# Recurrence of an RWKV layer: crossed factor products on four squares of the array, and a step's order staggered by groups of four tiles

## The reference

```python
def wkv_scan(r, decay, k, v, a_vec, b_vec, s0, reverse):
    def step(s, inp):
        r_t, w_t, k_t, v_t, a_t, b_t = inp
        sa = jnp.einsum('bhvk,bhk->bhv', s, a_t)
        s = s * w_t[:, :, None, :] + sa[..., None] * b_t[:, :, None, :] + v_t[..., None] * k_t[:, :, None, :]
        return s, jnp.einsum('bhvk,bhk->bhv', s, r_t)
...
for d in range(N_DIRS):
    reverse = d == 1
    yc_d, s_ctx = wkv_scan(r_c, dec_c, k_c, vh_c, -kk_c, kk_c * a_c, s0, reverse)
    yx_d, _ = wkv_scan(r_x, dec_x, k_x, vh_x, -kk_x, kk_x * a_x, s_ctx, reverse)
```

## Time and profile before

| | |
|---|---|
| three runs | 3694.95, 3694.49, 3689.80 us; median 3694.49 |
| profiled execution | 3690.83 us, span of its trace 3689.0 us, granted clock 0.98 |
| busy in the span | TensorE 3437.3 us (93%), weight loads 2264.5 (61%), VectorE 1475.1 (40%), ScalarE 1100.6 (30%), GpSimd 320.7 (9%) |
| chain that ended last | TensorE 76%, VectorE 10%, DMA 8%, ScalarE 3%, GpSimd 2% |
| recurrence | from about 1283 to 1776 us of the span |

### The profile page before, as it was taken

One profiled execution on the slowest core, in us unless ns is written; L12 is line 12 of the kernel. 1 busy time (PEld: TensorE's weight loads), 2 busy tenths in 40 slices (PEclk: granted clock), 3 DMA queues, 4 the chain that ended last, 5 costly groups with the idle time before them and its releaser, 6 DMA issues.

```text
span 3689.0 us, 64299 instructions
## 1 busy us (share of the span) xinstructions
PE 3437.3 (93%) x28700; PEld 2264.5 (61%) x28700; DVE 1475.1 (40%) x2584; ACT 1100.6 (30%) x2075; POOL 320.7 (9%) x264
## 2 busy tenths in 40 slices
PE   6999999999899999999778887899999999999998
PEld 4555344335558588888443332266888876878886
DVE  2133001013642277777540000157753435674343
ACT  3121111113442255544210000144532323543131
POOL 0001000000100234443110000001000001000000
PEclk9999999999799999999989999999999999999999
DMA  8237988996434334332528999920243312133320
GB/s 343 92 138 277 375 333 330 380 346 247 159 121 155 108 81 97 74 72 50 183 108 368 421 414 421 420 83 28 65 148 95 99 41 76 41 126 103 91 91 23
DMA packets 340516, 666.55 MB, mean 181 GB/s; under 512 B 156600, under 2 KB 250296, under 8 KB 284944
## 3 DMA queue, kind: packets, MB, share of 16 engines
q1 hardware_dynamic: 330128, 633.14, 47.8%
q10 hardware_dynamic: 6912, 18.88, 1.4%
q0 software_dynamic: 3200, 10.42, 0.8%
HBM read 630.92 MB, written 31.46 MB: 180 GB/s over the span
## 4 chain that ended last, share of the span: by engine, by line
PE 76%; DVE 10%; DMA 8%; ACT 3%; POOL 2%; issue 1%; SPq 0%; DVEq 0%; ACTq 0%; POOLq 0%
PE ps L1074 14%; PE ps L1079 5%; DMA ring<-in_moe_wu 4%; PE ps L716 4%; PE ps L3205 3%; PE ps L3204 3%; PE ps L3203 3%; PE ps L3221 3%; PE ps L3222 3%; PE ps L3220 3%; PE ps L632 3%; PE ps L633 3%; PE ps L634 2%; PE ps L1509 2%; PE ps L1534 2%; POOL ring L1899 2%
## 5 line engine op out<-in xcount | busy, mean ns | idle before, releaser
L1074 PE MATMUL ps<-ring,H 128*64 128x512 f32 x2016 | 482.8, 600 | 43.4 <-DMA ring<-in_moe_wu 33.0
L1185 DVE TENSOR_TENSOR scr<-ps,scr 128x512 f32<-128x512 f32 x32 | 22.1, 692 | 901.0 <-PE ps L1079 495.6
L1074 PEld LDWEIGHTS ps<-ring,H 128*64 128x64 f32 x2016 | 147.2, 137 | 321.9 <-issue 230.1
L1074 PE MATMUL ps<-ring,scr 128*64 128x512 f32 x1016 | 246.2, 601 | 31.2 <-DMA ring<-in_moe_wd 27.2
L3185 DVE TENSOR_TENSOR ring_rounded<-ring,scr_rounded 128x2048 fp32r<-128x2048 f32 x64 | 146.7, 2293 | 216.6 <-ACT scr_rounded L3178 216.3
L3220 PE MATMUL ps<-scr_rounded,ring_rounded 128*128 128x512 f32 x512 | 201.8, 394 | 1.6 <-DVE ring_rounded L3185 1.6
L3203 PE MATMUL ps<-scr_rounded,ring_rounded 128*128 128x512 f32 x512 | 202.8, 396 | 0.0
L3205 PE MATMUL ps<-scr_rounded 128*128 128x512 f32 x512 | 202.6, 396 | 0.0
L3222 PE MATMUL ps<-scr_rounded 128*128 128x512 f32 x512 | 202.4, 395 | 0.0
L3204 PE MATMUL ps<-H_rounded,scr_rounded 128*128 128x512 f32 x512 | 202.3, 395 | 0.0
L3178 ACT ACTIVATE scr_rounded<-ring 128x2048 fp32r<-128x2048 f32 x64 | 122.2, 1909 | 242.7 <-PE ps L3222 242.7
(11 more groups left out here) (524 smaller groups left out, 6793.2 us busy)
## 6 DMA issues: line engine op xcount, KB each, us to landing
ring<-in_moe_wu SPq DMA_DIRECT2D x128, 1024.0 KB, 9.2
ring<-in_moe_wd SPq DMA_DIRECT2D x127, 1024.0 KB, 9.5
ring<-in_moe_wg SPq DMA_DIRECT2D x124, 1024.0 KB, 9.2
ring<-in_mlp_w SPq DMA_DIRECT2D x64, 1024.0 KB, 5.4
ring<-in_ada_w SPq DMA_DIRECT2D x48, 1024.0 KB, 10.5
ring<-in_w_in SPq DMA_DIRECT2D x14, 1024.0 KB, 5.3
ring<-in_w_out SPq DMA_DIRECT2D x8, 1024.0 KB, 5.2
st_kka<-scr ACTq DMA_DIRECT2D x16, 384.0 KB, 3.5
```

What stands on the lines that cost most here:

```text
L1074: ins = pe.matmul(bx[64 * n:64 * n + 64, :], stat_x(k), w[:, k % 4, :], start=k == 0, stop=k == KT - 1)
```

## The change

It has four parts, all in the recurrence.

1. **Four squares.** `factor` on TensorE takes both units of a step together, tile by tile, and writes the reverse unit's product to the other half of the partitions (`rows(q ^ d)`): the forward unit stays on one diagonal of the array, the reverse unit goes to the other. ScalarE uncrosses it with two copies of 64 partitions.
2. **Groups.** Every call takes one group g for both units. In a level the order is factor of group 0, another product, update of group 0, factor of group 1, another product, update of group 1. The other products (outputs, states, keys, score products) come in halves; right side and solution stand first in the step.
3. **Scan, exponentials, operands.** CS has a second buffer (`CS1`) for odd units from u = 3 on. The first exponential (`chunk_rise`) and the second (`chunk_fall`) have their own marks, and so have the operands that read EP (`chunk_readers`) and those that are written with EN (`chunk_writers`). The scans move ahead: one to the start of the step, one to the end of level 1.
4. **The engines' own orders** follow: additions and transposes of VectorE by group for both units, the decay between the two halves of level 2, masked copies in pairs of banks, copies of ScalarE by group.

The core of the diff (waits of unchanged form are left out):

```diff
-            def factor(pair, l):
+            def factor(pair, l, g):
+                both = []
                 for u, d, c, img, first in pair:
...
+                    both.append((u, d, b))
+                for j in range(4 * g, 4 * g + 4):
+                    o = slice((j % 4) * CH, (j % 4) * CH + CH)
+                    for u, d, b in both:
+                        for q in range(2):
+                            ins = pe.matmul(b[rows(q ^ d), o], NM[d][l][rows(q), j, :], XT[d][rows(q), j, :],
                                             start=True, stop=True)
-                        did(T_, ins.then_inc(tensor_done, 1), f"G{u}.{l}.{g}")
+                        if j == 4 * g + 3:
+                            did(T_, ins.then_inc(tensor_done, 1), f"G{u}.{l}.{g}")
...
         def wkv_scalar(act):
+            def factor(pair, l, g):
+                for u, d, c, img, first in pair:
+                    t = pairs(tile(act, f"G{u}.{l}.{g}"))
+                    out = GT[d][:, 4 * g:4 * g + 4, :]
+                    if d == 0:
+                        did(A_, act.activation(out, t, ACT.Copy).then_inc(scalar_done, 1), f"free.G{u}.{l}.{g}")
+                    else:
+                        did(A_, act.activation(out[rows(0)], t[rows(1)], ACT.Copy).then_inc(scalar_done, 1))
+                        did(A_, act.activation(out[rows(1)], t[rows(0)], ACT.Copy).then_inc(scalar_done, 1), f"free.G{u}.{l}.{g}")
...
+                right_side(before, 0)
+                right_side(before, 1)
+                solution(before, 0)
+                factor(now, 1, 0)
+                solution(before, 1)
+                factor(now, 1, 1)
                 if after:
+                    chunk_rise(act, *after[0])
+                    chunk_fall(act, *after[0])
+                factor(now, 2, 0)
...
+                    chunk_rise(act, *after[1])
+                factor(now, 2, 1)
+                factor(now, 3, 0)
...
+                factor(now, 3, 1)
...
+                    keys(*now[1])
                 if after:
+                    chunk_fall(act, *after[1])
+                factor(now, 4, 0)
+                if after:
+                    chunk_evict(act, *after[0], (0,))
...
+        def csum(u):
+            return CS1 if u >= 2 and u % 2 else CS0
...
+        def chunk_readers(dve, u, d, c, img, first):
+            ld = LD[:, d]
+            if later(dve, f"rise{u}"):
+                dve.wait_ge(*at(f"rise{u}"))
...
+            did(V, dve.scalar_tensor_tensor(r[:, :, 0, :], v3(ld[:, 2, :]), -1.0, EM[d], ALU.mult, ALU.mult).then_inc(vector_done, 1))
+            if img:
+                did(V, dve.tensor_tensor(r[:, :, 1, :], v3(ld[:, 5, :]), EP[d], ALU.mult).then_inc(vector_done, 1))
+            e = CH - 1 if d == 0 else 0
+            did(V, dve.tensor_copy(PT[:, u % 4, :], EP[d][:, :, e]).then_inc(vector_done, 1))
...
+                right_side(before, 0)
+                right_side(before, 1)
+                solve(before, 0)
+                solve(before, 1)
+                factor(now, 1, 0)
+                factor(now, 1, 1)
+                outputs(image, 0)
+                update(now, 1, 0)
+                outputs(image, 1)
+                update(now, 1, 1)
+                factor(now, 2, 0)
+                states(before, 0)
+                update(now, 2, 0)
...
+                factor(now, 4, 0)
                 if after:
-                    chunk_products(pe, *after[0])
-                factor(now, 5)
-                update(now, 5)
+                    chunk_products(pe, *after[0], (0,))
+                update(now, 4, 0)
+                factor(now, 4, 1)
                 if after:
-                    chunk_products(pe, *after[1])
+                    chunk_products(pe, *after[0], (1,))
+                update(now, 4, 1)
...
```

More of the change, by code:

```diff
@@ L1981, in chunk_products @@
             w = 128 if img else CH
-            for g in range(2):
+            for g in groups:
                 for q in range(2):
@@ L2014, in solution, with keys @@
                     marks[f"free.S{u}.{g}"] = (A_, count[A_])
+            def keys(u, d, c, img, first):
+                for q in range(2):
+                    t = tile(act, f"T{u}.{q}")
+                    did(A_, act.activation(odd(BKT[d], q), t.rearrange("p (h c) -> p h c", c=CH), ACT.Copy).then_inc(scalar_done, 1), f"free.T{u}.{q}")
             steps = list(units())
@@ L2160, in keys @@
-            def keys(pair):
-                for u, d, c, img, first in pair:
-                    for q in range(2):
-                        b = bank(pe, f"T{u}.{q}")
-                        for j in range(8):
-                            ins = pe.transpose(b[:, j * CH:j * CH + CH], BK[d][rows(q), j, :, :], ident[rows(q), rows(q)])
-                        did(T_, ins.then_inc(tensor_done, 1), f"T{u}.{q}")
-            def right_side(pair):
+                    b = bank(pe, f"P{u}.{l}.{g}")
@@ new lines, in update @@
+                    if later(pe, f"free.G{u}.{l}.{g}"):
+                        pe.wait_ge(*at(f"free.G{u}.{l}.{g}"))
+                    if later(pe, f"xi{u}.{l - 1}.{g}"):
+                        pe.wait_ge(*at(f"xi{u}.{l - 1}.{g}"))
+                    for j, q, o in each(g):
+                        ins = pe.matmul(b[rows(q), o], GT[d][rows(q), j, :], x[rows(q), j, :],
+                                        start=True, stop=True)
+                    did(T_, ins.then_inc(tensor_done, 1), f"P{u}.{l}.{g}")
@@ L2169, in right_side, with keys @@
+            def keys(u, d, c, img, first):
+                for q in range(2):
+                    b = bank(pe, f"T{u}.{q}")
+                    for j in range(8):
+                        ins = pe.transpose(b[:, j * CH:j * CH + CH], BK[d][rows(q), j, :, :], ident[rows(q), rows(q)])
+                    did(T_, ins.then_inc(tensor_done, 1), f"T{u}.{q}")
+            def right_side(pair, g):
                 for u, d, c, img, first in pair:
@@ L2217, in states @@
-            def states(pair):
+                    b = ybank[u]
+                    if later(pe, f"free.S{u}.{g}"):
+                        pe.wait_ge(*at(f"free.S{u}.{g}"))
+                    for j, q, o in each(g):
+                        if later(pe, f"free.A{u}.{2 * g + q}"):
+                            pe.wait_ge(*at(f"free.A{u}.{2 * g + q}"))
+                        ins = pe.matmul(b[rows(q), o], sv[q][:, j, :], sc[:, 2 * j + q, CH:2 * CH],
+                                        start=False, stop=j == 4 * g + 3)
```

341 lines of the change are left out of this document (166 added, 175 removed).

## The result

The changed kernel takes 3673.9 us (median of 7 runs, 3667.0 to 3682.0) against 3694.5 of the kernel before in the same series: ratio 0.995, 95% interval 0.9939 to 0.9961. It is faster by 20 us (14 to 23 by the interval); forecast were 40, with 3654 in place of 3673.9. The direction was right and the time inside the range; the size was off by a factor of two.

The account below looks back on a forecast made before the run. TensorE was taken to set the recurrence's step, VectorE next. 55 saved on factor blocks less 12 for borders and 1 for waits is 42, shaded to 40 for scans: 3654 us, range 3632 to 3686.

Parts of the forecast that it names:

- Four squares, 55 saved: Factor products on TensorE: 120 blocks fall from 0.98 to 0.52 us each, 55 us saved, ends 0 and 59.
- feed of 25 ns: Rival, factor blocks: passes fed no faster than 25 ns, a block takes 0.80 us, 3665 us in all; chance 0.16.
- bank rule: Factor products: row halves cannot write one PSUM bank together, so no gain there; two-squares rival 3685 us, chance 0.09.
- Borders 12: TensorE, recurrence: some 110 more borders between kinds of product at 0.11 us each, 12 us lost, ends 0 and 15.
- waits 36: TensorE's waits in the new order: 36 us over twelve steps against 34.7 today, 1 lost; ends 22 gained, 40 lost.
- bank wait of 1.3: Level 4's second updates wait 1.3 us a step for first-score-product banks that VectorE's masked copies free.
- Loads and scans: Scans at a step's start: loads have 11 us left to land, cost nothing; scans beside masks nothing, other end 26 us.
- Twelve equal steps: Recurrence: blocks counted as 120 over twelve steps, waits as 2.9 a step, some 3.2 in context steps.
- cover of the crossed copies: ScalarE's 120 more copies, 4.0 us a step, are hidden by updates and filler, except level 1 of context steps.
- The lock: Rival: VectorE's six operand products, slipping beside GpSimd's masks, take 1.07 us extra each, 3731 us; chance 0.04.

Follow-up runs that it names:

- two squares: Changed kernel's order with both units' factor products on one diagonal and one ScalarE copy for two, against the changed kernel: 3688.3 us, ratio 0.999.
- First scans late: Changed kernel with VectorE's scans behind level 2 and level 3, ScalarE's exponentials behind them, in step 0 alone: 3670.1 us, ratio 0.9941.
- the loads issued first as well: Changed kernel with step 0's scans moved back and the second step's loads issued ahead of the 1 MB of weights: 3665.5 us, ratio 0.9928.
- last pairs: Changed kernel with levels 4 and 5 of the last step run as factors, factors, updates, updates: 3674.3 us, ratio 0.9949.
- solve between: Changed kernel with the second half of the solve between level 1's two factor blocks in image steps: 3680.2 us, ratio 0.9965.
- scans late in all steps: Changed kernel with the scans behind level 2 and level 3, exponentials behind them, in every step: 3709.1 us, ratio 1.0044.
- one alone: Kernel before, in its order, with only the factor products interleaved on both diagonals and ScalarE's crossed copies: 3713.4 us, ratio 1.0056.

## Why the forecast was right in direction and wrong in size

*Four squares, 55 saved.* The pace was as forecast. From the last pass of the updates ahead to the first of the next line, a block takes 0.61 us, and 1.08 with two squares in the same order: 0.47 saved where 0.46 was forecast, though the 32 passes mostly start within 0.52 us and not within 0.5. The rivals by a feed of 25 ns and by the bank rule are both out: two units' products write both halves of two banks at this pace. The term's worth was overstated: ten blocks give TensorE 4.7 us a step, and the steady step is 1.5 shorter. Two squares in the new order were to cost 31 us more (3685 for 3654) and cost 14.4. What the blocks no longer take, TensorE waits: 0.5 us of an image step of 40.9 are not busy with two squares, 1.9 of 38.9 with four.

*Borders 12, waits 36.* The stagger was understated. Two squares in the new order were to gain 0.8 a step (waits from 34.7 to 13, less 12 for borders) and gain 1.8 in an image step. A border is as forecast, 0.15 us from a line's last pass to the next line's first against a pace of 0.03. The two errors cancel, which is luck, and the steady step came out at 39.35 where 39.2 was forecast; the walk's bank wait of 1.3 is 0.8 in the trace, and its 0.3 to 0.7 elsewhere 0.4 to 0.6. TensorE's 37.0 busy us were put at 35, which is 39.5 less 4.6 for the blocks and leaves out the ten more borders of the forecast's own sum, 1.1.

*Loads and scans: here the forecast failed.* "I cost them at nothing" looked at a steady step. In step 0 the loads that the next scans read are issued only as the recurrence begins, and the scan now stands ahead of level 1's additions, which nothing of these loads concerns:

```profile
DVE scr L1960 <- DMA H<-st_kk: 12.1, 2, 11.6
```

In the kernel before, VectorE waited 2.3 us for that load:

```profile
DVE scr L1945 <- DMA H<-st_kk: 2.3, 1, 2.3
```

"First scans late" takes the wait out of the first stretch, but shows no gain clear of noise; with the loads issued first as well, the medians give 8.4 us and the profiled recurrence 4.6. So 5 to 8 us of this term's loss are shown by a run. The stretch itself is 9.1 us longer than before.

*Twelve equal steps.* The last step has no products of a next one to stand between. Four waits of 0.48 for ScalarE (1.9 us), stops of 1.10 and 1.53, and a clock at half for one stretch (0.88 over its second half) outweigh the shorter blocks: 4.2 us more. Its own experiment, last pairs, did not shorten it, so how these share the loss is open. The cover of the crossed copies was claimed for every step but level 1 of the context steps.

*The account.* 42 us for twelve steps are 3.5 a step. The first and the last stretch together make one step: counted as 3.5 less, they are 9.1 + 4.2 = 13.3 more, 16.8 of the 21.5 that are missing. The four context intervals were to give 14.0 and gave 10.2, the seven image ones 24.5 and gave 23.5; that is the other 4.8.

*VectorE and GpSimd.* The lock is real and hit other operations than those named. The six operand products take 0.65 to 0.68, as forecast, also L1957's, which took 1.22 in the mean before. The scans went from 1.22 to 1.60 us in the mean and the identity's add from 1.21 to 1.49; a decay beside the masks took up to 1.77. What the steady step pays for it is not shown: taking the scans out from beside the masks brought waits for ScalarE that cost more. In the context steps TensorE waited for transposes behind the decay.

*What was not foreseen at all.* Late code: 8 us more of stops than before, in 18 stops where there were 3. They lie inside the intervals of the account and are no further term. That they take part of what another edit gives is likely, but their sum also varies by 6 us between kernels with the same products.

*Left open.* TensorE's clock in the context steps. The changed kernel's profile shows 0.95 in one of them. Two variants whose instructions there are its own, last pairs and solve between, show 0.80 in the third interval, which lasts 43.1 us for 37.1:

```profile
1369.70:1412.80 43.10, 39.49 (x995) 37.40 (x993) 28.90 (x57) 26.05 (x66) 20.76 (x15) 0.80 0.35 77
```

0.80 lies between the two levels of 1.2 and 2.4 GHz: part of the interval ran at the lower. Just ahead of it TensorE had waited 2.15 us there, and 1.98 in the other variant, for VectorE's transposes, where the changed kernel waited 0.77; two squares, whose waits in these steps are 1.0 at most, stayed at 1.00. That makes the waits the likely cause, and it would account for the spread of the runs (15 us for the changed kernel, 6 before). It was not tested by itself.

## What to carry to other kernels

Do not multiply a steady step: walk the first and the last one of a loop by themselves, and for each instruction moved ahead ask when its inputs arrive in the first. A faster block of products pays only as far as other work stands between it and the engines that read it; measure both halves of such a change alone, since here one alone lost 21 us, the other alone gained 4, and together they gained 20. When TensorE stops with nothing to wait for at matmuls whose numbers lie at equal distances, look at its code.

## What the runs showed of the hardware

- Four 64x64 squares of the array run at once over whole blocks: four fp32 passes start each 0.06 us, 15 ns a pass, for 32 passes (0.48 to 0.52 us), with two banks written in both halves of the partitions. The Trainium skill's page "TensorE: Matmul & The Clock Gate" (section "Wait — 56ns, not 53.3ns?") says that start-to-start never drops below about 25 ns; across squares, this trace says otherwise.
- TensorE's code comes in pieces of 16 KB, some 126 matmuls (with their weight loads) each, and TensorE stops for 0.2 to 2.5 us when a piece lands late. It goes on 1.2 to 1.8 us after the landing (once 2.8). The recurrence has 2.3 us of such stops before and 4.4 with two squares, but 8.2 to 16.9 in the variants that have both the four squares and the new order, apart from scans late in all steps, which is slower and has 7.3.
- Beside GpSimd's masks, VectorE's operations on 128x512 elements in SBUF are held up whatever their form: add 1.49 us in the mean as tensor_tensor and 1.48 as scalar_tensor_tensor (0.67 at the least, in the kernel before), scan 1.20 alone and 1.60 beside them. Its additions that read PSUM took 0.42 in the mean, as before.
